# A hybrid decoder trunk: four tensors of a head pair reach token partitions by VectorE and DRAM instead of TensorE

## The reference

```python
sa = jnp.einsum('bhij,bhj->bhi', S, a_t)
S = S * w_t[:, :, None, :] + sa[..., None] * b_t[:, :, None, :] + v_t[..., None] * k_t[:, :, None, :]
y = jnp.einsum('bhij,bhj->bhi', S, r_t)
```

## Time and profile before

| | |
|---|---|
| runs | 1226.7, 1223.07, 1227.12 us |
| profiled execution | 1224.12 us, its span 1222.4 us |
| TensorE matmul busy | 1145.7 us, 94% of the span |
| VectorE, ScalarE, GpSimd busy | 529.3, 425.6, 205.6 us |
| the eight pairs | 61 to 440 us |
| mean granted TensorE clock | 0.991 of full |

### The profile page before, as it was taken

One profiled execution on the slowest core, in us unless ns is written; L12 is line 12 of the kernel. 1 busy time (PEld: TensorE's weight loads), 2 busy tenths in 40 slices (PEclk: granted clock), 3 DMA queues, 4 the chain that ended last, 5 costly groups with the idle time before them and its releaser, 6 DMA issues.

```text
span 1222.4 us, 29472 instructions
## 1 busy us (share of the span) xinstructions
PE 1145.7 (94%) x12520; PEld 627.1 (51%) x12520; DVE 529.3 (43%) x1004; ACT 425.6 (35%) x823; POOL 205.6 (17%) x234
## 2 busy tenths in 40 slices
PE   6999999999999999999997789999999999998785
PEld 5365555555555644555554445444554555554442
DVE  6756555564664511511111125899941511111125
ACT  5335355454453422211111124655443321111113
POOL 2000000000000000222221110788700122221110
PEclk9999999999999989999999999999999999999999
DMA  4017111011013078699999988226502899999996
GB/s 161 3 55 297 60 42 42 22 57 42 20 59 125 21 278 329 250 400 421 423 422 422 423 363 330 69 83 259 226 1 74 323 357 421 421 421 423 423 402 259
DMA packets 53779, 281.97 MB, mean 231 GB/s; under 512 B 14956, under 2 KB 17132, under 8 KB 36496
## 3 DMA queue, kind: packets, MB, share of 16 engines
q1 hardware_dynamic: 43952, 263.73, 53.7%
q0 software_dynamic: 9408, 16.32, 3.7%
q10 hardware_dynamic: 288, 0.03, 0.0%
HBM read 265.84 MB, written 30.41 MB: 242 GB/s over the span
## 4 chain that ended last, share of the span: by engine, by line
PE 73%; DMA 19%; DVE 3%; ACT 2%; issue 1%; SPq 1%; DVEq 0%
PE psum L1602 15%; DMA big<-in_moe_w_gate_up_dram 11%; PE psum L968 10%; PE psum L2136 9%; PE psum L2431 8%; PE psum L1783 6%; DMA h<-rows 5%; PE psum L981 4%; DMA h<-in_moe_w_gate_up_dram 3%; PE psum L1907 1%; PE psum L935 1%; PE psum L1772 1%; PE psum L2441 1%; PE psum L2407 1%; PE psum L1933 1%
## 5 line engine op out<-in xcount | busy, mean ns | idle before, releaser
L968 PE MATMUL psum<-big 128*64 128x256 f32 x1536 | 188.7, 388 | 25.9 <-DMA big<-in_moe_w_gate_up_dram 13.3
L1602 PE MATMUL psum<-big 128*128 128x512 f32 x384 | 191.1, 618 | 1.4 <-ACT big L1653 0.2
L968 PEld LDWEIGHTS psum<-big 128*64 128x64 f32 x1536 | 105.9, 138 | 90.6 <-issue 25.9
L1102 DVE SCALAR_TENSOR_TENSOR big<-psum,big 128x128 f32<-128x128 f32 x64 | 22.5, 351 | 299.9 <-ACT big L1052 299.9
L981 PE MATMUL psum<-big 128*64 128x512 f32 x512 | 120.9, 593 | 1.2 <-DMA big<-in_moe_w_down_dram 0.8
L2136 PE MATMUL psum<-big 128*128 128x512 f32 x256 | 116.2, 607 | 0.8 <-ACT big L2534 0.8
L888 POOL DMA_INDIRECT chosen<-big x60 | 59.8, 997 | 320.0 <-ACT big L1063 151.9
L1976 ACT COPY big<-psum 128x512 f32<-128x512 f32 (+1 forms) x112 | 69.2, 649 | 105.2 <-PE psum L1783 102.8
L2376 POOL TENSOR_TENSOR big<-big 128x512 f32<-128x512 f32 x76 | 96.7, 1272 | 36.0 <-ACT big L2516 25.5
L2431 PE MATMUL psum<-big,conv_w 128*128 128x512 f32 x224 | 96.5, 592 | 0.0
L1783 PEld LDWEIGHTS psum<-big 64*64 64x64 f32 x4096 | 71.5, 134 | 47.4 <-issue 46.4
(11 more groups left out here) (290 smaller groups left out, 1398.4 us busy)
## 6 DMA issues: line engine op xcount, KB each, us to landing
big<-in_moe_w_gate_up_dram SPq DMA_DIRECT2D x40, 2048.0 KB, 31.6
big<-in_moe_w_down_dram SPq DMA_DIRECT2D x64, 1024.0 KB, 30.6
conv_w<-in_moe_w_gate_up_dram SPq DMA_DIRECT2D x8, 2048.0 KB, 30.1
h<-in_moe_w_gate_up_dram SPq DMA_DIRECT2D x8, 2048.0 KB, 32.2
big<-in_moe_w_gate_up_dram SPq DMA_DIRECT2D x16, 1024.0 KB, 11.9
big<-in_rwkv_w_rkv_dram SPq DMA_DIRECT2D x24, 512.0 KB, 4.3
chosen<-h SPq DMA_DIRECT2D x8, 1024.0 KB, 12.4
conv_w<-in_conv_w_pw_dram SPq DMA_DIRECT2D x8, 1024.0 KB, 4.8
```

What stands on the lines that cost most here:

```text
L968: last = nc.tensor.matmul(o[half * SLOTS:(half + 1) * SLOTS, 0:F_EXP].rearrange("p (u f) -> p u f", u=2), m.xT[e // 2 % 2][:, c, (e % 2) * ...
L1602: last = nc.tensor.matmul(bank[b], m.w[:, n, c, :], x[:, c, :], start=(c == 0), stop=(c == C - 1))
```

## The change

1. VectorE turns `kt`, `at`, `bt` and `v` in blocks of 32x32 (`dve_turn`), writing with a step of four elements into the places of `u4`, `v2`, `l4` and `v1`, which are free then. The keys of pair q + 1 are turned behind `c1` of pair q; v right after ScalarE has copied it.
2. SyncE stores the turned blocks to DRAM, 14 transfers for the keys and 4 for v, in pieces of 512 bytes, and loads them back with tokens on partitions, one transfer of 768 KB and one of 256 KB. Both stand at the head of each pair in its queue.
3. `turn`, `flip` and the copies of their results are gone. The moved tensors are read as `x[half, hd, :, cp]`, with a step of four elements, both as weights and as moving operand.
4. On TensorE the products with `at` and `bt` open the pair; `L4`, `ub`, `v2` and the rest stand in a new order, and the product with the values (`lv`) comes after `l8`.
5. VectorE waits for the loaded values before it writes `v1`, ScalarE for the loaded keys before it writes `l4`. The centring of v now works in SBUF, after `v2` and the mask of ub, and the output of the pair before (`dve_moment_out`) behind it.
6. Some semaphores of the convolution stage are shared with finished ones of this stage, which changes no order.

```diff
@@ -1234,11 +1236,16 @@
-                (self.att, self.btt, self.ktt, self.vt) = (dead.take(CP, P) for _ in range(4))
+                self.moved = dead.take(3, CP * P)
+                (self.att, self.btt, self.ktt) = (self.moved[:, x].rearrange("p (h j c) -> p h j c", h=2, c=CP)
+                                                  for x in range(3))
+                self.moved_values = dead.take(CP * P)
+                self.vt = self.moved_values.rearrange("p (h j c) -> p h j c", h=2, c=CP)
+                self.turned = [x.rearrange("p h c t -> p (h c t)") for x in (self.u4, self.v2, self.l4, self.v1)]
...
@@ -1363,6 +1372,46 @@
+            KEY_STORES, VALUE_STORES = 16 * (4 + 6 + 4), 16 * 4
+
+            def quarter(x, s):
+
+                return x[32 * s:32 * s + 32].rearrange("r (q n) -> r q n", n=P)
+
+            def by_tokens(x, s):
+
+                return x.rearrange("(q r) (s n) -> s r q n", r=32, n=P)[s]
+
+            def store_keys(q):
+                kt, at, bt = m.turned[0:3]
+                to_at, to_bt, to_kt = (turned_keys[q % 2, x] for x in range(3))
+                sp.wait_ge(m.kt_turned.sem, m.kt_turned.by(q))
+                for s in range(4):
+                    sp.dma_start(by_tokens(to_kt, s), quarter(kt, s)).then_inc(m.keys_stored, 16)
+                sp.wait_ge(m.at_turned.sem, m.at_turned.by(q))
+                for s in range(2):
+                    sp.dma_start(by_tokens(to_at, s), quarter(at, s)).then_inc(m.keys_stored, 16)
+                for s in range(2, 4):
+                    for par in range(2):
+                        sp.dma_start(by_tokens(to_at, s)[:, 2 - 2 * par:4 - 2 * par],
+                                     quarter(at, s)[:, 2 * par:2 * par + 2]).then_inc(m.keys_stored, 16)
+                sp.wait_ge(m.bt_turned.sem, m.bt_turned.by(q))
+                for s in range(4):
+                    sp.dma_start(by_tokens(to_bt, s), quarter(bt, s)).then_inc(m.keys_stored, 16)
+
+            def store_values(q):
+                sp.wait_ge(m.v_turned.sem, m.v_turned.by(q))
+                for s in range(4):
+                    sp.dma_start(by_tokens(turned_values[q % 2], s), quarter(m.turned[3], s)).then_inc(m.values_stored, 16)
+
+            def load_moved(q):
+                sp.wait_ge(m.keys_stored, KEY_STORES * (q + 1))
+                if q:
+                    sp.wait_ge(m.z_ps.sem, m.z_ps.by(q - 1))
+                sp.dma_start(m.moved, turned_keys[q % 2].rearrange("x p n -> p x n")).then_inc(m.keys_in, 16)
+                sp.wait_ge(m.values_stored, VALUE_STORES * (q + 1))
+                sp.dma_start(m.moved_values, turned_values[q % 2]).then_inc(m.values_in, 16)
+
...
             for q in range(1, PAIRS - 2):
+                store_keys(q)
+                store_values(q)
+                load_moved(q)
                 sp.wait_ge(m.l_ps.sem, m.l_ps.by(q))
                 load_v(q + 1)
...
+        def dve_turn(x, to, done):
+
+            nc.vector.transpose(to.rearrange("p (e n u) -> p u e n", u=CP, n=32),
+                                x.rearrange("p (u e n) -> p u e n", u=CP, n=32)).then_inc(done.now(), 1)
+
+        def dve_turn_keys(m, dve, q):
+            dve_wait(dve, q, m.kt_ready)
+            dve_turn(m.kt, m.turned[0], m.kt_turned)
+            dve_wait(dve, q, m.at_ready)
+            dve_turn(m.at, m.turned[1], m.at_turned)
+            dve_wait(dve, q, m.bt_ready)
+            dve_turn(m.bt, m.turned[2], m.bt_turned)
+
         def pe_moment_var(m, pe, p, places):
...
             def tok(x):
-                return lambda hd, cp, par: x[half(par), cp, hd * HD:(hd + 1) * HD]
+                return lambda hd, cp, par: x[half(par), hd, :, cp]
             def swapped_tok(x):
-                return lambda hd, cp, par: x[half(par ^ hd), cp, hd * HD:(hd + 1) * HD]
+                return lambda hd, cp, par: x[half(par ^ hd), hd, :, cp]
             wait(m.rk_ready)
-            turn(m.at, 0, 1)
-            turn(m.bt, 256, 0).then_inc(m.abt_ps.now(), 1)
-            flip(m.kt, 5, m.ktt_ps)
-            wait(m.v_ready)
-            flip(m.v, 2, m.vt_ps)
+            product(m.bt, m.at, 4, 0, 1)
+            product(m.at, m.bt, 4, 256, 1).then_inc(m.l_ps.now(), 1)
+            product(m.kt, m.at, 2, 0, 0)
+            product(m.kt, m.rt, 2, 256, 0).then_inc(m.lk_ps.now(), 1)
             if before:
                 pe_moment_var(m, pe, p, VARIANCES)
             head_sums(m.heads, m.rk, BONUSES).then_inc(m.bonus_ps.now(), 1)
+            wait(m.v_ready)
             if more:
                 if before:
                     pe_wait(pe, m.g_ready.sem, m.g_ready.by(p))
                 pe_prepare_low_rank(m, pe, nq)
-            wait(m.btt_ready, m.ktt_ready)
-            product(m.bt, m.at, 4, 0, 1)
-            product(m.at, m.bt, 4, 256, 1).then_inc(m.l_ps.now(), 1)
-            wait(m.vt_ready)
-            product(m.kt, m.at, 2, 0, 0)
-            product(m.kt, m.rt, 2, 256, 0).then_inc(m.lk_ps.now(), 1)
+            wait(m.masked_l)
+            crossing(swapped(m.ld), swapped(m.ud), 4, 0, CH, 0)
+            crossing(swapped(m.ud), swapped(m.ld), 4, 256, CH, 0).then_inc(m.l2_ps.now(), 1)
             if more:
                 pe_prepare_k(m, pe, nq, 0, 4)
             else:
-                mix_first(1, 0, 1)
-
-            wait(m.masked_l)
-            crossing(swapped(m.ld), swapped(m.ud), 4, 0, CH, 0)
-            crossing(swapped(m.ud), swapped(m.ld), 4, 256, CH, 0).then_inc(m.l2_ps.now(), 1)
+                mix_first(1, 0, 2)
+            wait(m.l2_ready, m.u2_ready)
+            crossing(mat(m.l2), mat(m.u2), 4, 0, CH, 1)
+            crossing(mat(m.u2), mat(m.l2), 4, 256, CH, 1).then_inc(m.l4_ps.now(), 1)
+            wait(m.bv_ready)
             if before:
                 pe_wait(pe, m.var_read, q)
             product(m.bt, m.rt, 6, 256, 0).then_inc(m.ub_ps.now(), 1)
             if more:
-                pe_prepare_k(m, pe, nq, 4, C)
+                pe_prepare_k(m, pe, nq, 4, 6)
             else:
-                mix_first(1, 1, 3)
-            wait(m.l2_ready, m.u2_ready)
-            crossing(mat(m.l2), mat(m.u2), 4, 0, CH, 1)
-            crossing(mat(m.u2), mat(m.l2), 4, 256, CH, 1).then_inc(m.l4_ps.now(), 1)
-            wait(m.l2_plus, m.v1_ready, m.bv_ready)
+                gate()
+            wait(m.l2_plus, m.v1_ready, m.ub_ps)
             crossing(mat(m.l2p), mat(m.v1), 6, 0, CH, 1).then_inc(m.v2_ps.now(), 1)
+            if more:
+                pe_prepare_k(m, pe, nq, 6, C)
+            else:
+                mix_first(1, 2, 3)
+            wait(m.u4_ready, m.l4_plus, m.v2_ready)
+            crossing(swapped(m.l4p), swapped(m.v2), 4, 0, CH, 0).then_inc(m.v4_ps.now(), 1)
+            wait(m.masked_ub)
+            crossing(swapped(m.u4), swapped(m.l4), 6, 0, CH, 0).then_inc(m.l8_ps.now(), 1)
             wait(m.masked_lk)
+            wait(m.vt_ready)
             crossing(mat(m.lak), tok(m.vt), 2, 0, CH, 1).then_inc(m.lv_ps.now(), 1)
             if more:
-                pe_prepare_r(m, pe, nq, 0, 2)
+                pe_prepare_r(m, pe, nq, 0, 4)
             else:
-                gate()
-                mix_first(1, 3, 4)
-            wait(m.u4_ready, m.l4_plus, m.v2_ready)
-            crossing(swapped(m.l4p), swapped(m.v2), 4, 0, CH, 0).then_inc(m.v4_ps.now(), 1)
-            crossing(swapped(m.u4), swapped(m.l4), 6, 0, CH, 0).then_inc(m.l8_ps.now(), 1)
-            if more:
-                pe_prepare_r(m, pe, nq, 2, 4)
-            else:
-                mix_first(1, 4, 5)
+                mix_first(1, 3, 5)
             wait(m.v4_ready, m.l8_plus)
             crossing(mat(m.l8p), mat(m.v4), 4, 0, CH, 1).then_inc(m.dt_ps.now(), 1)
             if more:
...
@@ -2076,7 +2122,14 @@
             w(m.lk_ps)
             TTn(m.mrk, four(two_banks(2, 256, 256)), mask(m.upper_incl), ALU.mult).then_inc(m.masked_lk.now(), 1)
+            w(m.bonus_ps, m.v_ready)
+            for bonus, p_, t in straightened(BONUSES):
+                last = TTn(m.bv[p_, t], bonus, m.v[p_, t], ALU.mult)
+            last.then_inc(m.bv_ready.now(), 1)
+            w(m.l2_ready)
+            TTn(m.l2p, m.l2, mask(m.eye), ALU.add).then_inc(m.l2_plus.now(), 1)
             w(m.masked_l)
+            dve.wait_ge(m.values_in, 16 * q + 16)
...
@@ -2084,16 +2137,20 @@
             last.then_inc(m.v1_ready.now(), 1)
             if more:
                 dve_prepare_decays(m, dve, nq)
-            w(m.ub_ps)
-            TTn(m.mrb, four(two_banks(6, 256, 256)), mask(m.upper_incl), ALU.mult).then_inc(m.masked_ub.now(), 1)
-            w(m.l2_ready)
-            TTn(m.l2p, m.l2, mask(m.eye), ALU.add).then_inc(m.l2_plus.now(), 1)
-            if before:
-                dve_moment_out(m, dve, p)
-            w(m.l4_ready)
+            w(m.l4_ready, m.v1_ready)
             TTn(m.l4p, m.l4, mask(m.eye), ALU.add).then_inc(m.l4_plus.now(), 1)
             w(m.v2_ps)
```

(14 more changed lines are left out.)

142 lines of the change are left out of this document (70 added, 72 removed).

## The result

The changed kernel takes 1274.1 us (median of 4 runs, 1268.6 to 1276.2) against 1225.1 us: a ratio of 1.039, 95% interval 1.0355 to 1.0425. It is 49 us slower. The prediction named 1230 and a range of 1219 to 1245, so it was wrong by 44 us, though its sign was right.

What follows compares the result with a forecast made beforehand. TensorE's work was taken to bound a middle pair. Terms +3.7 + 10.4 - 9.0 - 0.3 = +4.8 us gave 1228.9 on the profiled 1224.1, 1231.5 on the median 1226.7; it named 1230, range 1219 to 1245.

Steps and rivals of the forecast that it cites:

- the sum of the prediction: Whole kernel: the terms of pair 0, pair 1, middle pairs and pair 7 together, +4.8 us.
- A rule weighed: TensorE's 176 matmul records a pair that read operands with a step of four elements: priced at 0.
- The upper bound: TensorE's strided records: doubled time of all 176, +2.9 us a pair, 23 us in all.
- Rival 2: Strided operands cost TensorE time: half the bound gives 1241 us, the full bound 1253; chance 0.20.
- Pair 0, +3.7: First pair: no rest for the turns, stores begin later, values in at 15.0, dt ends 3.7 us later.
- Pair 1, +10.4: Second pair: stores queue behind 8 MB of fills, +9.4 us, plus 1 for a lower clock.
- Middle pairs, -9.0 in five: Pairs 2 to 6: each gains 1.8 us; together -9.0, range -5.5 to -10.5.
- sign of being wrong altogether: Middle pairs on TensorE: the prediction is wrong altogether if they are no shorter than 47 us.
- rival 4: DRAM writes or reading them back take longer: 2 us more give +15, 1243 us or more; chance 0.11.
- Its sign: Middle pairs: VectorE waiting for the values in every one by more than 1 us.
- Pair 7, -0.3: Last pair: fewer fills and no scan, dt at 17.6 against 17.9; -0.3 us, range -1.4 to +0.5.
- A slack of 0.3 us: Middle pairs: TensorE wants the centred values at 16.0, they exist at 16.2; it waits 0.3 us.

Runs made afterwards that it cites:

- e2: The kernel before, with only the layout of att, btt, ktt and vt changed, so they are written and read with a step of four elements; 1246.6 us.
- e7: The changed kernel with the fills issued behind pair 1's loads, the turned values in their own tile and VectorE's wait moved to ahead of the reduction; 1245.7 us.
- e12: e7 with ScalarE copying the loaded keys into contiguous order, centred values written contiguous, and ScalarE waiting for key stores only ahead of L fourth; 1229.5 us.
- e1: The changed kernel with TensorE reading contiguous elements of the moved tensors instead of elements four apart, so wrong operands; 1268.9 us.
- e4: The changed kernel with e1's contiguous, wrong operands and the fills of chosen issued behind pair 1's stores and loads; 1258.0 us.
- e5: The changed kernel without its stores to DRAM, both loads fetching output weights instead of keys and values, operands still strided; 1246.0 us.
- e6: e5 with the operands from the loaded tiles read as contiguous elements; 1228.2 us.
- e10: Like e12, but GpSimd makes the key copies, and three of four output weight loads are issued behind pair 7's stores and loads; 1244.5 us.
- e16: e12 with the values loaded ahead of the keys in every pair, and in pair 0 stored ahead of bt's; 1233.5 us.

## Why the prediction was wrong, point by point

Two terms failed, of about the same weight. The pairs up to the router exceed the sum of the prediction by 47 us. About 21 of them are the step of four elements, priced at 0 (2.6 us in each of eight pairs). The round trip of the values, with VectorE's chain behind it, was priced too short: that is 15 in the five middle pairs, 4 in pair 0 and 2 in pair 1. What is left is pair 7's.

- **A rule weighed: strided operands priced at 0.** The nearer row (transposes that kept their pace with strided weights) was of another size, 128 columns at 130 ns a record; here a record takes 16 ns. That the size is why the transposes kept their pace is not shown. The upper bound, 23 us, was right: e2 measured 22.6, and e7 to e12 gave 16.2 back, where ScalarE also waits for less. Rival 2 was half of the truth; its 1253 is this cost alone.
- **Pair 0, +3.7: measured +10.5.** The path was the one that the prediction took, key stores, values, lv; its terms were short. The values came in 18.0 us after the pair's start, not 15.0 (all key stores were issued 10.1 us after the start, not 8.3; the value load then had to wait until the value stores had landed, and was issued at 15.4). TensorE waited 5.64 us for v1 and then ran two projections at the lower clock, 3.78 us for 1.98, and lv began 7.8 us behind the values instead of 6.5. The stride adds 2.7. The wait for v1 was not forgotten time: by the prediction's own numbers v1 would be ready at 16.3 and lv's turn on TensorE come at 19.9, ahead of the centred values at 21.5.
- **Pair 1, +10.4: measured +14.7.** The mechanism was right: VectorE waited 15.8 us for the DMA of the values (12 to 15 predicted). The size was off by the stride, 2.6, and by the stores' slow issue behind the fills: the values were in at 26.4 us instead of 24.4. The clock shows in two rows of projections, 4.93 us for 3.70 and 3.33 for 1.98.
- **Middle pairs, -9.0 in five: measured +19.3.** The prediction's own sign of being wrong altogether, no middle pair under 47 us, came true: 50.1 to 52.8. The retiming of TensorE holds: without stores and stride, 45.9 us. With the stride it is 48.4, and the rest, 1.7 to 4.4 us a pair, is the values: in after 10.2 to 13.4 us for 9.7, and lv 7.0 to 7.3 us behind them for 6.5 (turns 1.1 for 0.7, reduction 1.1 for 0.7). So lv began 17.3 to 20.7 us after the pair's start, where the prediction had 16.3; over the five pairs this makes 15 us, and the stride 13. That is rival 4. Its sign, VectorE waiting for the values in every middle pair by more than 1 us, came true with 3.0 to 6.2 us, but was badly chosen: VectorE asks for them at 7.2, so 9.7 alone would have given 2.5.
- **Pair 7, -0.3: measured +8.0** (to the long row of the output product). TensorE waits 4.58 us for v1, pays 2.6 us for the stride and has one stop of 0.88 us. That TensorE can stop with nothing to wait for was in none of the cases.
- **Costs that hide each other.** Removing the stride gave 5 us in e1, 3 in e4 (both within their intervals) and 18 between e5 and e6; removing the wait gave 15.5. The sum of single removals is not the price of the change.

The 1.5 us later start of pair 0 does not come from the order of the pairs: e2, with the old order, starts at 62.7 too, and e6, e10, e12 and e16, with the new one, at 61.0 to 61.4. In every kernel that starts late the first group of eight 128x256 records of the preparation (L1518 before, L1579 after) takes 3.4 to 3.8 us, in every other 2.0.

Three things stay open: what makes that group slow; how the price divides where both operands have the step, ktt with vt (with one such operand, moving or as weights, the groups show it alone); and why ScalarE's wait for the keys is as long as it is and whether it costs anything. Nor is there a place in the instruction stream at which e12 was measured below the 1225 us of the kernel before. Its pair 0 alone still costs 5.4 us.

## What to carry to other kernels

When a layout change leaves an operand with a step, price the step on every product that reads it, at the products' own pace, before anything else is added up. For each wait added, list what stands behind it on its engine and move the wait down to the first item that needs the data: here moving it from ahead of v1 to ahead of the reduction was worth 15.5 us. A slack of 0.3 us carries no small errors; here the load's landing alone varied by 3 us from pair to pair. Judge a change of a few us in a kernel of densely issued small products only after shifting the instruction stream, since that alone moved the kernel before by 8 us.
